# Position bias inside the compression products, bias tables fetched a stage earlier, and output rows transposed inside the last projection

## The reference, cut to what matters

```
hid = jnp.einsum('jd,jde->e', pe, w1) + part[0, :, 0:nc]
hid = hid + part[1, :, 1:1 + nc]        # part = segments of 16 keys times the two halves of w1
out = jnp.einsum('bnge,ed->bngd', jax.nn.gelu(hid), w2)
```

## Time and profile before

| what | us |
|---|---|
| median of three runs | 1875.83 |
| the profiled execution, its own time | 1881.08 |
| its span, first to last instruction | 1879.3 |
| PE busy, of the span | 1772.3 (94%) |
| DVE / ACT / POOL busy | 816.1 / 525.9 / 702.7 |
| mean granted TensorE clock, of full speed | 0.956 |

### The profile page before, as it was taken

How to read it: one execution, slowest core, us unless ns; L and a number is a source line. 1 busy time by engine, 2 the same in 40 slices (tenths; PEclk the granted TensorE clock), 3 DMA queues, 4 the chain that set the end, 5 groups by cost and what they waited for, 6 DMA issues and landing times. The chain is left out here.

```text
span 1879.3 us, 35977 instructions
## 1 busy us (share of the span) xinstructions
PE 1772.3 (94%) x15724; PEld 1685.5 (90%) x15724; DVE 816.1 (43%) x1650; ACT 525.9 (28%) x896; POOL 702.7 (37%) x282
## 2 busy tenths in 40 slices
PE   6989788789978998999999999999999999999997
PEld 6987677559856997899999999999999999999997
DVE  4162487223483444465530355443246455024421
ACT  5132365223331222322221222322223222112211
POOL 1200000013213111465553465656565565445541
PEclk8987699889979998899999999999999999999999
DMA  5640330423201000222223222332222222232222
GB/s 146 111 70 23 128 100 24 124 76 92 74 9 47 4 4 27 68 68 90 84 68 96 90 69 64 95 104 75 90 86 72 88 70 74 85 100 81 74 71 77
DMA packets 158252, 140.84 MB, mean 75 GB/s; under 512 B 16170, under 2 KB 153806, under 8 KB 157710
## 3 DMA queue, kind: packets, MB, share of 16 engines
q1 hardware_dynamic: 158094, 138.53, 25.2%
HBM read 132.62 MB, written 10.02 MB: 76 GB/s over the span
## 5 line engine op out<-in xcount | busy, mean ns | idle before, releaser
L271 POOL TENSOR_TENSOR w_lo<-w_raw,w_hi 128x2048 fp32r<-128x2048 f32 (+3 forms) x109 | 458.8, 4209 | 798.8 <-ACT w_hi L265 798.6
L310 PE MATMUL ps<-h_hi,w_hi 128*128 128x288 f32 x1792 | 385.1, 296 | 0.0
L310 PE MATMUL ps<-h_lo,w_hi 128*128 128x288 f32 x1792 | 384.6, 295 | 0.0
L310 PE MATMUL ps<-h_hi,w_lo 128*128 128x288 f32 x1792 | 384.4, 295 | 0.0
L265 ACT ACTIVATE w_hi<-w_raw 128x2048 fp32r<-128x2048 f32 (+3 forms) x109 | 190.0, 1743 | 510.1 <-PE ps L310 460.0
L310 PEld LDWEIGHTS ps<-h_hi,w_hi 128*128 128x128 f32 x1792 | 287.2, 188 | 0.3
L310 PEld LDWEIGHTS ps<-h_lo,w_hi 128*128 128x128 f32 x1792 | 287.2, 188 | 0.0
L310 PEld LDWEIGHTS ps<-h_hi,w_lo 128*128 128x128 f32 x1792 | 287.0, 188 | 0.0
L419 DVE TENSOR_TENSOR xT<-ps,xT 128x576 f32<-128x576 f32 x48 | 35.7, 757 | 265.9 <-PE ps L310 265.9
L310 PE MATMUL ps<-g_hi,w_hi 128*128 128x288 f32 x704 | 151.1, 295 | 0.0
L310 PE MATMUL ps<-g_lo,w_hi 128*128 128x288 f32 x704 | 151.0, 295 | 0.0
(11 more groups left out here) (500 smaller groups left out, 3016.3 us busy)
## 6 DMA issues: line engine op xcount, KB each, us to landing
w_raw<-in_ffn_up SPq DMA_DIRECT2D x44, 1024.0 KB, 5.1
w_raw<-in_ffn_down SPq DMA_DIRECT2D x16, 768.0 KB, 4.8
w_raw<-in_w_in_odd SPq DMA_DIRECT2D x12, 1024.0 KB, 5.1
w_raw<-in_ffn_down SPq DMA_DIRECT2D x16, 640.0 KB, 4.4
w_raw<-in_w_in_even SPq DMA_DIRECT2D x7, 1024.0 KB, 5.4
w_raw<-in_w_in_even SPq DMA_DIRECT2D x6, 872.0 KB, 9.9
BT<-rv SPq DMA_DIRECT2D x8, 520.0 KB, 3.5
seg<-in_cache_cmp_kv SPq DMA_DIRECT2D x32, 128.0 KB
```

What stands on the lines that cost most here:

```text
L271: pool.tensor_tensor(slab_view(wlo[slot], st), slab_view(raw[slot], st), slab_view(whi[slot], st).bitcast(F32), ALU.subtract).then_inc(w_l ...
L310: last = pe.matmul(ps[:, bank + 2 * j + half, 0:HT], w[slot][:, c:c + 128], x[:, xs + t, half * HT:(half + 1) * HT], start=(t == 0 and n = ...
```

## The change

Five edits. (a) `bias_of` goes. The position vector becomes one more column of `KTc` of group 0 (columns 288 and 289, set to zero before), written by DVE, and group 0's products run over 289 columns instead of 288; ACT copies the bias out of column 288 of the result once that product is done. (b) The copies of `kNew` and `vc` move from the end of DVE's list to the end of ACT's. (c) The first two `BT` loads move from the start of the prompt block to the end of the compression block's SP list. (d) The sample block's table loads move into the prompt block's SP list at head 2, and their two memsets into DVE's list there. (e) `store_all` goes; a new function `residual_out` takes the last projection, and transposes, copies and stores within it.

```diff
+        def residual_out(st, hhi, hlo, first):
...
+            pair_of = lambda f: 2 + 4 * (f % 2)
+            slots = lambda f: [n for n in range(2 * f, min(2 * f + 2, len(new_states)))]
...
+            def sync(sp):
+                for g in range(2, 8):
+                    load_slab(sp, st, 0, g, 16)
+                count = 0
+                for lo, hi in ((0, 4), (4, 7), (7, 8)):
+                    sp.wait_ge(yt_d, hi)
+                    sp.dma_start(yp[:, :, 128 * lo:128 * hi], yt[:, 0:4, 128 * lo:128 * hi]).then_inc(y_out, 16)
+                    sp.wait_ge(yt_a, hi)
+                    sp.dma_start(ys[:, 128 * lo:128 * hi], yt[0:NS, 4, 128 * lo:128 * hi]).then_inc(y_out, 16)
+                    for f in range(lo, hi):
+                        for n in slots(f):
+                            for a0, a1, target in new_states[n][2]:
+                                sp.dma_start(target, rows[n][a0:a1, :]).then_inc(st_out_sem, 16)
+                                count += 16
...
+                def taken(f):
+                    b = pair_of(f)
+                    act.wait_ge(yt_ps, f + 1)
+                    for m, n in enumerate(slots(f)):
+                        r = new_states[n][1]
+                        act.copy(rows[n][0:r, :], ps[0:r, b + 1, 128 * m + 128:128 * m + 256])
+                    act.copy(yt[0:NS, 4, 128 * f:128 * f + 128], ps[0:NS, b + 1, 0:128]).then_inc(yt_a, 1)
+                for g in range(1, 8):
+                    split_hi(act, st, 0, g, 16)
+                    if g >= 2:
+                        taken(g - 2)
...
+            def tensor(pe):
+                def rows_of(f):
+                    b = pair_of(f)
+                    pe.wait_ge(x_last, f + 1)
+                    if f >= 2:
+                        pe.wait_ge(yt_d, f - 1)
+                        pe.wait_ge(yt_a, f - 1)
+                    for m, n in enumerate(slots(f)):
+                        pe.transpose(ps[0:new_states[n][1], b + 1, 128 * m + 128:128 * m + 256], new_states[n][0], ident[:, :])
+                    pe.transpose(ps[0:NS, b + 1, 0:128], xT[:, f, TP:T], ident[:, :])
+                    for t in range(4):
+                        last = pe.transpose(ps[:, b, 128 * t:128 * t + 128], xT[:, f, 128 * t:128 * t + 128], ident[:, :])
+                    last.then_inc(yt_ps, 1)
+                for g in range(8):
+                    def ready(pe, t):
+                        if g == 0:
+                            first["ready"](pe, t)
+                        elif t == 5:
+                            rows_of(g - 1)
+                    products(pe, st, 0, g, 16, 4 * (g % 2), 0, hhi, hlo, ready)
+                rows_of(7)
...
+            def load_bias(sp, h):
+                sp.dma_start(BT[h % 2][:, :], bass.AP(rv_dram.tensor, h * RVL, [[1, 128], [1, BTW]])).then_inc(bt_in, 16)
...
                     sp.wait_ge(gate_in, 128)
+                    sp.wait_ge(hid_done, 4)
+                    load_bias(sp, 0)
+                    load_bias(sp, 1)
+                    sp.wait_ge(bt_in, 32)
...
                         for gg in range(2):
+                            n = 289 - gg
                             for i in range(16):
-                                last = pe.matmul(ps[:, 4 + gg, 0:288], w1[:, i, :], KTc[:, gg, i % 8, i // 8:i // 8 + 288],
+                                last = pe.matmul(ps[:, 4 + gg, 0:n], w1[:, i, :], KTc[:, gg, i % 8, i // 8:i // 8 + n],
...
-                        act.wait_ge(peb_ps, 3 + kv)
-                        act.copy(pe_bias[:, kv:kv + 1], ps[:, 7, 64 + kv:65 + kv]).then_inc(act_chain.sem, 1)
+                        act.wait_ge(hid_done, 2 * kv + 1)
+                        act.copy(pe_bias[:, kv:kv + 1], ps[:, 4, 288:289]).then_inc(act_chain.sem, 1)
...
+                    def position_column(kv):
+                        dve.tensor_copy(KTc[:, 0, :, 288:290], peT[:, kv, :].rearrange("p (h i) -> p i h", h=2))
...
                         if n == 3:
                             dve.wait_ge(hid_done, 2)
+                            if u == 0:
+                                position_column(1)
...
                         if h >= 2:
                             sp.wait_ge(s_taken, 4 * (h - 1))
-                        src = bass.AP(rv_dram.tensor, h * RVL, [[1, 128], [1, BTW]])
-                        sp.dma_start(BT[h % 2][:, :], src).then_inc(bt_in, 16)
-                        sp.wait_ge(bt_in, 16 * (h + 1))
+                            load_bias(sp, h)
+                            sp.wait_ge(bt_in, 16 * (h + 1))
+                        if h == 2:
+                            sp.dma_start(wm[:, :], k["wmask"]).then_inc(tab_in, 16)
+                            for s2 in range(2):
+                                sp.dma_start(SBs[64 * s2:64 * s2 + 64, :],
+                                             bass.AP(rv_dram.tensor, RV0 - TP, [[RVL, NH], [-1, TS], [1, TP]])).then_inc(tab_in, 16)
+                            sp.wait_ge(tab_zero, 1)
+                            for s2 in range(2):
+                                for grp in range(4):
+                                    c0 = TS * (2 * grp + s2)
+                                    sp.dma_start(SBn[64 * s2:64 * s2 + 64, grp, c0:c0 + TS],
+                                                 bass.AP(rv_dram.tensor, RV0, [[RVL, NH], [-1, TS], [1, TS]])).then_inc(tab_in, 16)
...
                     masked_max(0)
                     masked_max(1)
+                    dve.memset(SBn[:, :, :], NEG)
+                    dve.memset(SBc[:, :, :], NEG).then_inc(tab_zero, 1)
```

More of the change, by code:

```diff
@@ L431, in residual, with scalar, gpsimd, vector @@
             return dict(sync=sync, act=scalar, pool=gpsimd, pe=tensor, dve=vector)
+        def residual_out(st, hhi, hlo, first):
+            base_g = st["base"]
+            reg = Region(R)
+            yt = reg.take("yt", [128, 5, D])
+            rows = [reg.take("rows", [128, 128]) for _ in range(16)]
+            assert reg.at <= G0
+            x_last, yt_ps, yt_a, yt_d, y_out = sem("x_last"), sem("yt_ps"), sem("yt_act"), sem("yt_dve"), sem("y_out")
+            pair_of = lambda f: 2 + 4 * (f % 2)
+            slots = lambda f: [n for n in range(2 * f, min(2 * f + 2, len(new_states)))]
+            yp = o["y_prompt"][0].rearrange("(t p) d -> p t d", p=128)
+            ys = o["y_sample"].rearrange("b t d -> (b t) d")
+            def sync(sp):
[12 more added lines that the diff above has]
+                                count += 16
+                sp.wait_ge(y_out, 96)
+                sp.wait_ge(st_out_sem, count)
+            def scalar(act):
+                def taken(f):
[9 more added lines that the diff above has]
+                        taken(g - 2)
+                taken(6)
+                taken(7)
+            def gpsimd(pool):
+                for g in range(1, 8):
+                    split_lo(pool, st, 0, g, 16)
+            def tensor(pe):
[19 more added lines that the diff above has]
+                rows_of(7)
+            def vector(dve):
+                def taken(f):
+                    dve.wait_ge(yt_ps, f + 1)
+                    dve.tensor_copy(yt[:, 0:4, 128 * f:128 * f + 128], ps[:, pair_of(f), :].rearrange("p (t d) -> p t d", t=4)).then_inc(yt_d, 1)
+                for g in range(8):
+                    b = 4 * (g % 2)
+                    x = xT[:, g, :].rearrange("p (a t) -> p a t", a=2)
+                    dve.wait_ge(slab_done, base_g + g + 1)
+                    dve.tensor_tensor(x, ps[:, b:b + 2, 0:HT], x, ALU.add).then_inc(x_last, 1)
+                    dve.wait_ge(x_last, g + 1)
+                    dve.nop().then_inc(banks_free[g % 2], 1)
+                    taken(g)
+            return dict(sync=sync, act=scalar, pool=gpsimd, pe=tensor, dve=vector)
@@ L710, in ffn @@
                 a1 = ffn_up(l, up1, fb, None)
-                d1 = residual(down1, ghi_d, glo_d, gain=gain, first=a1["first"])
+                if l == 0:
+                    d1 = residual(down1, ghi_d, glo_d, gain=gain, first=a1["first"])
+                else:
+                    d1 = residual_out(down1, ghi_d, glo_d, a1["first"])
                 ffn_states(l)
@@ L744, in _ @@
                         part["dve"](dve)
[L747 to L802, removed]
@@ L853, in even_mixer @@
             E2 = r.at
+            def load_bias(sp, h):
+                sp.dma_start(BT[h % 2][:, :], bass.AP(rv_dram.tensor, h * RVL, [[1, 128], [1, BTW]])).then_inc(bt_in, 16)
+            BT = [at("BT", [128, BTW], F32, E2 + 8192 + 4 * BTW * n) for n in range(2)]
+            bt_in = sem("bt_in")
             rs = r.take("rs", [128, 5, 12])
@@ L1282, in _ @@
                     pe.matmul(ps[:, 6, 384:480], flip[:, :], gp[:, 0:4, :].rearrange("p t n -> p (t n)"), start=True, stop=True).then_inc(gpr_ps, 1)
[L1284 to L1293, removed]
                     def segments(n):
@@ L1423, in _ @@
                         last.then_inc(q_ev, 1)
```

(19 more changed lines are left out.)

28 lines of the change are left out of this document (5 added, 23 removed).

## The result

The changed kernel takes 1857.72 us (median of seven executions, 1852.34 to 1863.58); the kernel before, run beside it, 1875.40 (seven, 1869.73 to 1880.97). The ratio is 0.9913, 95% interval 0.9887 to 0.9939: 16.3 us, or 17.7 by the medians, where 19.9 and 1856 were forecast. The profiled execution took 1855.83 us with a span of 1854.0, 25.3 less than the profiled one of before. That is more than the medians differ by, so the two profiles have to be split into stages before anything is read from their ends.

What follows compares the result with a forecast made beforehand. PE, busy 94% of the span, was taken as the bound; elsewhere its waits count. The terms 6.3 - 0.1 + 0.9 + 2.7 + 1.8 + 1.4 + 6.9 = 19.9 us took 1875.83 to 1855.9, say 1856, range 1848 to 1866.

Steps and rivals of the forecast that it cites:

- (a): Second hidden layer of the compression: without the bias products its first product starts at about 173.45, gaining 6.3 us.
- (b): End of the compression: DVE's list ends at 206.43 instead of 207.31 without the copies, gaining 0.9 us.
- (c): Start of prompt attention: DVE's first score no longer waits for the table's DMA, gaining 2.7 us.
- (d): Sample attention: DVE's scores start 1.8 us sooner and PE's wait for pages goes, gaining 1.4 us.
- (e): Last projection: 18.5 us of tail become 5.3 for transposes and 6.3 at the end, gaining 6.9 us.
- two bounds: Low clock in second hidden products: at best none, 2.3 us gained; at worst rising as before, 3.2 us lost.
- rival 1: Second hidden layer: the clock returns no earlier without the bias products, 3.2 us less gain, 1859; chance 0.14.
- The first pass: Compression, bias products beside DVE's splitting of the queries: PE would wait for DVE there instead, gain nothing.
- The row of the same operation: Last projection: 28 weight loads of such transposes take 3.10 us, 0.111 each, so 48 cost 5.3 us.
- the f32 records of the earlier trace: Four f32 records within an fp32r stream: upper bound of 0.24 us per transpose in the last projection, 11.5 us.
- Sum: Whole kernel: all terms together gain 19.9 us, from a median of 1875.83 to 1855.9 us.
- Rival 3: Prompt attention runs at half clock for longer; three more such heads would give 1897 us; chance 0.04.

Runs made afterwards that it cites:

- after's second profile: The changed kernel run once more with nothing altered, for a second profile; ratio to the kernel before 0.9915.
- the last, filled one: The changed kernel with products of no use put into PE's pauses at three places; 1849.54 us, ratio to the kernel before 0.9864.

## Why the prediction held, point by point

- **(a), 6.3 us.** From ACT's last `segT` to the first hidden product it was 179.81 - 173.34 = 6.47 us, and is 0.09: 6.4. The low stretch is as long as before and only earlier, which was the value taken between two bounds. The rule of the Trainium skill ("TensorE: Matmul & The Clock Gate", Part 1) led to rival 1. The runs with and without the bias products speak against that use of it here: 3.6 to 4.8 us with them, 3.0 to 4.3 without. The first pass gave nothing of its own: it starts hidden products 15.4 us after the first `q_st` step in both profiles. The compression's other 1.9 us I put down to clock: 26.0 us at half speed instead of 40.2, a figure that differs between profiles of one kernel (29.3 and 26.4 for (a) and (b) alone, 15.8 in after's second profile).
- **(b), 0.9 us.** Right in its own stage (9.7 to 8.8 us). The step that failed is the one not written: that nothing behind it depends on it. It costs 4.3 us in the heads.
- **(c), 2.7 us.** At its place exactly that (3.9 to 1.2 us). Left out: the sooner stores and table of head 2, and the clock. Without (b) it brought 7.4 in the heads, (b) and (c) together 3.1.
- **(d), 3.2 us.** 3.5 in the stage, which is 72.5 to 74.1 us in the eight profiles with (d) and 75.8 to 79.9 in the six without; DVE's first score and the pages came as forecast. The recurrence behind it takes 2.9 us more in after, and 320.2 to 320.7 in all kernels with (d) but the last, filled one (317.5). Yet one without (d) has 320.8 too, so I don't put it down to (d). It is open.
- **(e), 6.9 us.** 7.4, with 5.2 for the transposes (5.3 forecast) and 5.9 at the end (6.3). The row of the same operation was the right one to trust, over the f32 records of the earlier trace rows. One count in the working is wrong: SP issues 27 stores at the end of the kernel before, not 24, so an issue takes 14.75 / 27 = 0.55 us and not 0.61. With that the same sum gives 5.5 to 6.0 us from the last product to the end instead of 5.6 to 6.8; SP's eleven issues in after took 1851.01 - 1844.89 = 6.12 us, 0.56 each.
- **Sum.** By stages without the first block: 9.2 + 3.1 + 3.5 - 2.9 + 7.4 + 1.0 = 21.3, of which 1.9 is clock in the compression; forecast 19.9; measured 16.3 by the ratio, 11.4 to 21.2 by its interval.
- **Rival 3** had a chance of 0.04 and was ruled out for the whole change, rightly. But its mechanism is the strongest thing in these traces. In one of two profiles it ate the gain of (a) and (b) alone, and its mirror image added to (c). That the units "come in the same order after the same kind of pause" was no argument: (b), which takes 0.9 us from that pause, made 11 us of low clock into 22 in the profiles.

The forecast was right in the total partly because errors of both signs met: 2.9 us lost in the recurrence and 4.3 behind (b) stand against 4.7 more than forecast from (c) and 1.9 from the compression's clock. Each edit's own term, worked out from the row that ends last, was right within 0.5 us.

## What to carry to other kernels

Price an edit at its own wait, and then look at what runs after the pause that it shortens: where PE starts a stage at half clock, the time until the clock returns is worth as much as the wait. When a kernel's executions spread by 1%, compare stages cut at the same instructions and the granted clock of each, not totals. Short products of no use in pauses that PE has anyway are a cheap test of how much the clock costs. In the changed kernel they were a gain by themselves, in the kernel before they were not (1.0013), because the next table then held up the heads. A transfer that nobody waits for now may be hidden by a slow clock alone: find the next table in the queue before speeding up what stands ahead of it.

## What the runs showed of the hardware that I had not expected

- The same kernel's prompt attention stayed at 1.2 GHz for 46 us of its start in one execution and for 25 in another, with PE busy for nearly all of the longer stretch behind its first 11 us.
- 32 records of one-column products, 6.83 us with no gap, did not shorten the low stretch behind them (4.03 against 4.11 us), while in the last kernel 128-column products of no use over a pause of some 6 us kept the clock at 1.00 for the next 110 us, until 302.7.
- Transposes inside a stream of fp32r products cost 0.109 us each, no more than the 0.111 that the same transposes took back to back.
